# A hybrid decoder trunk on one core: near and far softmax parts weighted in their probabilities instead of in their outputs

## What is computed

```
def dilated_band_attention(q, k, v, bias, dilation):
    ...
    logits = jnp.where(key_ok[None, :, None, None, None, :], logits, NEG_INF)
    lse = jax.nn.logsumexp(logits, axis=-1)
    probs = jnp.exp(logits - lse[..., None]).astype(v.dtype)
    out = jnp.einsum('bnrhic,bncrhe->bnirhe', probs, vband).reshape(B, s_pad, H, Dh)[:, :S]
    ...
def dilated_attention_mixer(h, w_qkv, q_gain, k_gain, w_o, rel_bias):
    ...
    weights = jax.nn.softmax(jnp.stack(lses), axis=0)
    o = jnp.sum(weights[..., None] * jnp.stack(outs).astype(jnp.float32), axis=0)
    return o.reshape(B, S, ATTN_HEADS * ATTN_HEAD_DIM).astype(h.dtype) @ w_o
```

## Time and profile before

| | us |
|---|---|
| median of 3 runs | 1822.7 |
| lowest, highest | 1820.6, 1823.12 |
| the profiled execution: its time | 1820.68 |
| its span, first to last instruction | 1818.9 |
| PE busy | 1791.6 (99%) |
| DVE busy, ACT busy | 875.0 (48%), 759.4 (42%) |

### The profile page before, as it was taken

How to read it: one execution, slowest core, us unless ns; L and a number is a source line. 1 busy time by engine, 2 the same in 40 slices (tenths; PEclk the granted TensorE clock), 3 DMA queues, 4 the chain that set the end, 5 groups by cost and what they waited for, 6 DMA issues and landing times.

```text
span 1818.9 us, 36160 instructions
## 1 busy us (share of the span) xinstructions
PE 1791.6 (99%) x15618; PEld 1366.8 (75%) x15618; DVE 875.0 (48%) x1515; ACT 759.4 (42%) x1292; POOL 197.1 (11%) x172
## 2 busy tenths in 40 slices
PE   8999999999999999999999999999999999999999
PEld 3746666666478888888887887887887788888887
DVE  6724444454364444333455555555555544444322
ACT  4434444432242222222556656656657532323221
POOL 0033334331100000000111011111110000000000
PEclk9999999999999999999999999999999999999999
DMA  3321222131123323332232222222222233223332
GB/s 107 117 67 54 84 67 67 64 99 55 59 90 104 93 93 99 99 104 93 93 93 70 82 82 70 82 82 70 82 82 70 63 95 98 93 95 103 101 97 93
DMA packets 57541, 155.00 MB, mean 85 GB/s; under 512 B 5591, under 2 KB 22535, under 8 KB 57384
## 3 DMA queue, kind: packets, MB, share of 16 engines
q1 hardware_dynamic: 57288, 152.63, 26.4%
q10 hardware_dynamic: 96, 0.07, 0.0%
HBM read 150.51 MB, written 11.61 MB: 89 GB/s over the span
## 4 chain that ended last, share of the span: by engine, by line
PE 91%; ACT 4%; DVE 2%; issue 1%; POOL 1%; DMA 0%; ACTq 0%; DVEq 0%; POOLq 0%
PE bank L573 89%; PE bank L576 3%; ACT f L1597 2%; DVE f L2122 0%; DVE r L1994 0%; ACT f L1584 0%; ACT f L1610 0%; DVE f L1724 0%; DVE f L1727 0%; ACT r L1575 0%; DVE f L1744 0%; ACT r L1287 0%; DMA f<-const 0%; ACT f L1571 0%; DVE r L1750 0%
## 5 line engine op out<-in xcount | busy, mean ns | idle before, releaser
L573 PE MATMUL bank<-r 128*128 128x512 f32 x5424 | 1255.8, 391 | 2.7 <-DVE r L1994 1.1
L573 PEld LDWEIGHTS bank<-r 128*128 128x128 f32 x5424 | 1011.9, 188 | 226.0 <-issue 10.7
L573 PE MATMUL bank<-f 64*64 64x64 f32 (+5 forms) x9762 | 502.2, 255 | 16.0 <-ACT f L1312 4.3
L1701 DVE TENSOR_TENSOR r<-f,r 128x1024 fp32r<-128x1024 f32 x222 | 274.9, 1239 | 397.2 <-ACT r L1287 397.2
L573 PEld LDWEIGHTS bank<-f 64*64 64x64 f32 (+3 forms) x9762 | 306.9, 140 | 200.6 <-issue 128.0
L1287 ACT ACTIVATE r<-f 128x1024 fp32r<-128x1024 f32 x222 | 232.5, 1048 | 147.1 <-PE bank L573 141.5
L2314 POOL TENSOR_TENSOR r<-f,r 128x512 fp32r<-128x512 f32 x48 | 62.2, 1296 | 839.1 <-ACT r L1575 839.1
L1554 ACT ACTIVATE r<-f 128x512 fp32r<-128x512 f32 x44 | 27.8, 632 | 215.6 <-DVE f L2033 215.6
L2063 DVE TENSOR_TENSOR f<-bank,f 128x512 f32<-128x512 f32 x72 | 56.2, 781 | 73.3 <-PE bank L573 70.0
L1551 ACT ACTIVATE f<-f 128x512 f32<-128x512 f32 x44 | 27.8, 632 | 110.5 <-DVE f L2023 110.5
L1584 ACT ACTIVATE f<-bank,f 128x512 f32<-128x512 f32 x48 | 32.9, 686 | 94.8 <-PE bank L573 94.8
(11 more groups left out here) (106 smaller groups left out, 909.9 us busy)
## 6 DMA issues: line engine op xcount, KB each, us to landing
f<-stream SPq DMA_DIRECT2D x246, 512.0 KB, 3.4
bias_copies<-bias_rows SPq DMA_DIRECT2D x6, 1536.0 KB
f<-xT SPq DMA_DIRECT2D x16, 256.0 KB, 4.8
f<-lora_out SPq DMA_DIRECT2D x16, 128.0 KB, 6.4
f<-bias_copies SPq DMA_DIRECT2D x16, 128.0 KB, 3.2
f<-bias_copies SPq DMA_DIRECT2D x32, 64.0 KB, 2.9
outT<-f SPq DMA_DIRECT2D x8, 256.0 KB, 4.3
f<-const SPq DMA_DIRECT2D x1, 576.0 KB, 3.8
```

The source lines that it names most:

```text
L573: return nc.tensor.matmul(out, lhsT, rhs, start=start, stop=stop, skip_group_check=True)
L1701: TT(r(lo_at(q), 1024), f(O_RAW + panel_of(q) % RAW * 1024, 1024), rf(hi_at(q), 1024), ALU.subtract).then_inc(s["w_lo"], 1)
```

## The change

The two parts are weighted before they meet V, in the factor that the probabilities are multiplied with anyway. With own and other log-sum it is 1 / (sum * (1 + exp(other - own))). `attend` sums both into bank 6.

- A query's near log-sum lies in a tile of queries in a row, its far one in a tile of one residue. The near queries are now stored in the order (block, residue, index): `norm_projection` writes query group 0 in four instructions instead of one, SP loads its bias in four transfers of 32 partitions instead of one, and `attend` writes the far part as runs of 32.
- `total` (DVE, i = 5, ahead of everything of that step) makes all 16 log-sums of the pair at once. `exchange_lse` (PE, visit 5) takes the place of `lse_difference`: 4 matmuls with 128 x 128 weights and 16 columns each instead of 16 with 128 columns. `other_lse` (DVE, i = 5) is seven small instructions, each waiting for the one before, `weights` (ACT) one Exp, `scales` (DVE) two more. `normalize` of both halves stands behind them, at i = 5 and 6, where it stood at i = 2 and 4.
- Flips go through two banks, 5 and 7, one for a head; both heads of a group stand together. Flips and attends move: visits 6 and 7 flip groups 0 and 1, visit 8 attends 0 and 1 and flips group 2, visit 0 of the next iteration flips group 3, its visit 1 attends 2 and 3. Visit 4 is empty. Flips and attends now fill five visits (6, 7, 8, 0, 1).
- The sigmoid, its two table loads for an iteration, the copy `keep_near` and the three steps of the old `combine` go; ACT and DVE read bank 6 directly for high and low part.

```diff
-            def lse_difference(hp):
+            def exchange_lse(hp):
                 fill_att(4, "lse", hp)
...
-                for n in range(2 * NT):
-                    for h in range(2):
-                        lo = HD * h
-                        o = banks[4][lo:lo + HD, n * P:(n + 1) * P] if n < NT else \
-                            banks[4][lo:lo + HD, n - NT:S:4]
-                        last = mm(o, bc(f(O_SM + 40 * h + 32 + n, 1), (0, HD)), con(C_ID), n == 0, False)
+                pe.wait_ge(s["lse"], hp + 1)
...
+                for c in range(4):
+                    last = mm(banks[4][:, 16 * c:16 * (c + 1)], f(O_E4 + c * P, P), bc(f(O_SM + 32, 48), (40, 2), (1, 8)))
                 last.then_inc(s["lse_ps"], 1)
...
-                    if 3 <= i <= 6:
-                        flip_probs(a, 0, i - 3)
+                    if i == 0 and b >= 0:
+                        flip_probs(b, 3)
                     if i < 4:
                         logits(a, i)
-                    if 4 <= i <= 7:
-                        attend(a, i - 4)
-                    if 3 <= i <= 6:
-                        flip_probs(a, 1, i - 3)
-                    if i == 7:
-                        lse_difference(a)
+                    if i == 1 and b >= 0:
+                        attend(b, 2)
+                        attend(b, 3)
+                    if i == 5:
+                        exchange_lse(a)
+                    if i in (6, 7):
+                        flip_probs(a, i - 6)
+                    if i == 8:
+                        attend(a, 0)
+                        attend(a, 1)
+                        flip_probs(a, 2)
...
+            def weights(hp):
+                act.wait_ge(s["ex_step"], 7 * hp + 6)
+                A(f(O_EX + 112, 16), f(O_EX + 112, 16), ACT.Exp).then_inc(s["ex_exp"], 1)
...
+            def other_lse(hp):
+
+                def step(ins, n):
+                    ins.then_inc(s["ex_step"], 1)
+                    dve.wait_ge(s["ex_step"], 7 * hp + n)
+
+                dve.wait_ge(s["lse_ps"], hp + 1)
+                att_free(TT(bc(f(O_EX, 64), (4, 16), (1, 4)), banks[4][:, 0:64].rearrange("p (u n) -> p u n", n=4),
+                            bc(f(O_SM + 80, 4), (0, 16), (1, 4)), ALU.mult), 4)
+                att_read(dve, 4, "lse", hp)
+                step(TT(bc(f(O_EX + 64, 32), (2, 16), (1, 2)), bc(f(O_EX, 62), (4, 16), (1, 2)),
+                        bc(f(O_EX + 2, 62), (4, 16), (1, 2)), ALU.add), 1)
+                step(TT(f(O_EX + 96, 16), bc(f(O_EX + 64, 31), (2, 16)), bc(f(O_EX + 65, 31), (2, 16)), ALU.add), 2)
...
+                step(TS(f(O_EX + 112, 16), f(O_EX + 112, 16), 80.0, None, ALU.min), 5)
+                TS(f(O_EX + 112, 16), f(O_EX + 112, 16), -80.0, None, ALU.max).then_inc(s["ex_step"], 1)
...
             for it in range(NHP):
-                a = it - 1
+                a, b = it - 1, it - 2
                 for i in range(9):
+                    if a >= 0 and i == 5:
+                        total(a)
                     split_low(p_of(T_QKV + 9 * it + i) + LEAD)
                     take_projection(it, i)
                     if i:
                         norm_projection(it, i - 1)
...
-                    if i in (2, 4):
+                    if i == 3 and b >= 0:
+                        combine_low(b)
+                    if i == 5:
+                        other_lse(a)
+                        scales(a)
+                    if i in (5, 6):
                         for h in range(2):
-                            normalize(a, h, i // 2 - 1)
+                            normalize(a, h, i - 5)
```

More of the change, by code:

```diff
@@ L1146, in block_of, with flip_probs @@
                 return O_P + h * 4 * S + (n + (4 if kind == "B" else 0)) * 2 * P + e * P
[L1148 to L1153, removed]
+            def flip_probs(hp, g):
+                for h in range(2):
+                    b = 5 + 2 * h
+                    fill_att(b, g, hp)
+                    pe.wait_ge(s[f"probs{h}"], 8 * hp + (4 if g < 2 else 8))
+                    for j, what in enumerate(GROUPS[g]):
+                        last = flip(banks[b][:, j * P:(j + 1) * P], f(block_of(h, what), P))
+                    last.then_inc(s["flipped"], 1)
@@ L1625, in keep_near, with keep_both @@
[L1625 to L1630, removed]
+            def keep_both(a, g):
+                for h in range(2):
+                    keep_flipped(a, h, g)
             for it in range(NHP):
-                a = it - 1
+                a, b = it - 1, it - 2
                 for i in range(9):
[L1635 to L1640, removed]
+                    split_high(p_of(T_QKV + 9 * it + i) + LEAD)
@@ L1647, in _ @@
                         continue
[L1648 to L1651, removed]
+                    if i == 2 and b >= 0:
+                        combine(b)
                     if i in (2, 4):
@@ L1654, in _ @@
                             exps(a, h, i // 2 - 1)
[L1655 to L1659, removed]
+                    if i == 5:
+                        weights(a)
+                    if i == 8:
+                        keep_both(a, 2)
             def last_pair(a):
                 projection_aux(a, 8)
+                keep_both(a - 1, 3)
                 split_high(PAN_WO1 + 3)
+                combine(a - 1)
                 exps(a, 0, 0)
@@ L2074, in norm_projection @@
                     if hp >= 2 and g == 0:
-                        dve.wait_ge(s["attended"], 4 * (hp - 1))
+                        for h in range(2):
+                            dve.wait_ge(s[f"logits{h}"], 4 * (hp - 1))
                     to = O_QN + (hp % 2 * 6 + g * 2 + kind) * S
@@ L2080, in norm_projection @@
                             bc(f(O_QS), (4, P), (1, 4)), ALU.mult, ALU.mult).then_inc(s["qk_norm"], 1)
+                    elif kind == 0:
+                        for c in range(4):
+                            part = lambda off: bc(f(off + c, S - 3), (P, 4), (4, 32))
+                            last = STT(bc(f(to + 32 * c, S - 96), (P, 4), (1, 32)), part(O_QR + n % 2 * S), gain,
+                                       part(O_QS), ALU.mult, ALU.mult)
+                        last.then_inc(s["qk_norm"], 1)
                     else:
@@ L2152, in _ @@
                         continue
-                    if i == 0 and a:
-                        combine(a - 1)
                     if i < 4:
@@ L2183, in last_pair @@
                 negate_max(a, 1, 1)
-                normalize(a, 1, 0)
-                combine(a - 1)
-                normalize(a, 0, 1)
                 split_low(PAN_WO1 + 4)
-                normalize(a, 1, 1)
-                combine_low(a - 1)
-                combine(a)
+                total(a)
+                other_lse(a)
+                scales(a)
+                for half in range(2):
+                    for h in range(2):
+                        normalize(a, h, half)
                 combine_low(a)
```

183 lines of the change are left out of this document (88 added, 95 removed).

## The result

The changed kernel takes 1837.65 us (median of 4 runs, 1835.06 to 1840.76) against 1821.65 (1820.31 to 1823.12): ratio 1.008, 95% interval 1.0066 to 1.0095; the medians stand 16.0 us apart. The forecast was no change (1822.3, range 1815.6 to 1829.5). One rival had the right sign (small steps that cost more, slower), but not the mechanism.

What follows compares the result with a forecast made beforehand. PE, busy 1791.6 of 1818.9 us, was taken as the bound. Stretch 1 -14.4, rest of iterations +13.3, first pair -0.84, last iteration -2.25, last pair +3.8 made -0.4 us: 1822.3, no change, range 1815.6 to 1829.5.

Steps and rivals of the forecast that it cites:

- small steps that cost more: Rival, DVE/ACT chain: ten steps at 0.3 us each, +7 us, 1829.3; decides from 0.06 a step; chance 0.27.
- The logarithms on ACT: Stretch 1, both heads' Ln on ACT: ready 13.36 us after the start of product 4.
- The whole chain of ten: Dependent small steps from `other_lse` to the multiplications: seven on DVE, ACT's Exp, two more; T + 17.49 to T + 19.54.
- the flips' price: Exchange in visit 5: flips at 0.11 us each would make 0.87, the upper end; 0.65 was taken.
- -0.4 was forecast: Whole kernel: sum of all terms, -14.4 + 13.3 - 0.84 - 2.25 + 3.8 = -0.4 us.
- the savings named: Per iteration: 16 matmuls less exchange 1.1 us, old wait 0.6, fewer changes between dense, flip and attend some 0.65.
- the two waits of 2.75: New PE waits per iteration, for the exchange (1.79 us) and the multiplications (0.96), taking back the savings.
- 68.5 against 68.35: Length of one attention iteration in us, forecast for the changed kernel against that of the kernel before.
- stretch 1: Product 4's start to product 7's: 22.12 us in place of 24.18, -2.06 in each of seven iterations, -14.4.
- PE starts 0.15 after DVE's end: Stretch 1, visit 5: `total` ends at T + 13.56, so PE starts the exchange at T + 13.71.
- the second wait: Visit 6: PE waits 0.96 us, in two parts, for the multiplications of heads 0 and 1.
- waits of 1.79: Visit 5: PE waits 1.79 us for the exchange, since the visit 4 that covered this is empty.

Runs made afterwards that it cites:

- both causes out: Changed kernel with the exchange writing bank 5 instead of 4 and five needless dense matmuls ahead of it: 1824.08 us, ratio 1.0006.
- the two filled kernels: Changed kernel with ten needless dense matmuls ahead of the exchange, 1826.82 us; changed kernel with exchange in bank 5 and five such matmuls, 1824.08 us.
- the three kernels with cover: Changed kernel, older pair's two attends moved from visit 1 to 5: 1818.50 us; also exchange in bank 5: 1813.85; also product 4's norm behind near-half multiplications: 1810.56.
- the kernel with the other bank: Changed kernel with one edit, the exchange writes bank 5 instead of bank 4: 1828.22 us, ratio 1.0033.
- two others: Changed kernel with product 4's norm ahead of step 5's split on ACT, 1833.55 us; kernel before with a bare PE wait added behind visit 4, 1848.45 us.
- the other kernel: Kernel before with a PE wait for ACT's first far-half exponential added behind visit 4: 1848.45 us bare, 1836.58 with nine needless matmuls ahead of the wait.

## Why the prediction was wrong

**What held.** The logarithms on ACT were forecast 13.36 after product 4 and ended at 13.38 (1169.85). `total` was forecast to end at 13.56; it starts at 13.48 and ends at 13.65. The multiplications on DVE were forecast from 19.54 and start at 19.65 (1176.12). The small steps take 0.17 to 0.25 us, seven of them 1.5. The whole chain of ten took 2.31 (1173.81 to 1176.12) where 2.05 were forecast, 0.03 a step more, and began 0.15 early; the rival of dearer steps needed 0.06 a step and falls. The exchange cost 0.91 and not 0.65, at the flips' price. With both causes out the order costs +1.1 us where -0.4 was forecast. One sum doesn't come out: the savings named beside the two waits of 2.75 (1.1, 0.6 and 0.65) make 2.35, where 68.5 against 68.35 asks for 2.6. Nothing else was worked out from it.

**The step that failed is in stretch 1: "PE starts 0.15 after DVE's end".** It took the log-sums for the only thing that the exchange waits for. The code names a second, `fill_att(4, ...)`. In the kernel before it had cost nothing, but not because the bank was long free: in visit 7 `lse_difference` stood behind a norm too, that of product 6. There eight attends lay between (1111.90 + 1.03 = 1112.93), and ACT had been idle and read the bank at once, until 1112.69:

```profile
1112.00 0.69 ACT L1584 ACTIVATE f<-bank,f 128x512 f32<-128x512 f32 x1 [2.66 <-PE bank L573]
```

In visit 5 nothing lies between, and ACT reaches the norm's Ln only behind its exponentials and a split. The wait was 2.85 and not 1.79. Of the difference the second wait (0.96 forecast, 0 in the seven iterations) gave most back, and at full clock product 7 came 22.66 after product 4 instead of 22.12: some 3 us by the two filled kernels.

**The term that was missing is the clock: 11.9 us of the 16** by the medians (16.0 less 4.1), 10 of 14.6 by the ratios; their intervals leave some 3 us either way. The prediction counted a microsecond of waiting as a microsecond. It had the earlier trace rows with PE's waits at 0.62 and wrote down waits of 1.79 without asking whether a length is reached from which PE comes back slower. Among the kernels here the seven waits and the profiled execution's mean clock go together: 0.3 to 0.9 us with 0.998 or 0.999, 1.7 to 3.1 with 0.992 to 0.994, and between them the three kernels with cover (0.996 to 0.998), whose first iteration still waits for 1.8 or 2.7. It is not a rule for the single wait: behind 2.85 the clock fell in some iterations and not in others, and behind 1.16 it fell once. A wait of 1.79, as forecast, would have cost already: the kernel with the other bank has that wait, and with it filled by five matmuls it is 4.1 us faster (1828.22 and 1824.08, beside 1822.72 and 1823.01 for the kernel before).

The two causes don't simply add. With bank 4 the clock costs 11.9 us, with bank 5 only 4.1, since there a second wait takes up half of a slow product 6. So the bank alone is worth 3.0 with the clock held up and 9.4 without. With either of the two out the time would have been inside the stated range (1828.22 and 1826.82).

**That the new waits take back what the order saves** was right within what can be told: at full clock, with the other bank, an iteration takes 68.80 us, where 68.5 were forecast and 68.35 stood before. A way out was in the same paragraphs: visit 4 was emptied, while visit 1 got 16 attends that wait for nobody. Put ahead of the exchange they take 11.5 us of waiting (20.1 to 8.6) and most of the clock's share with it.

## What to carry to other kernels

Of a step that is moved, list every wait in front of it, the one for the buffer that it writes above all, and look up who used that buffer last at the new place, and what the engine that frees it has to do first. Where PE is busy all the time, price a new wait twice, once for itself and once for the clock behind it, less what a later wait takes up; needless matmuls in the wait tell in one experiment how much is the clock. And if an order has a wait of known length, move into it work that is ready.

## What the runs showed of the hardware

A PE that is 98% busy, and at full clock in the rest of the attention stage, ran dense matmuls at 1.2 GHz for part of the run behind a single wait of 1.7 to 3.1 us: in four of seven iterations of the changed kernel's profile, in five with the other bank, in six in each of two others. Behind waits of 0.3 to 0.95 us it never did, behind one of 1.16 it did once. It costs 11.9 us here, four times what the longer wait itself did, and 11.9 us again in the other kernel. It costs less where another wait follows: a product of 7.13 us instead of 5.71 cost nothing in front of two waits of 1.46 together. Ten needless matmuls of 0.23 us in an iteration made it 10.8 us faster (1837.65 and 1826.82). Four fp32 matmuls of 16 columns against 128 x 128 weights took 0.91 us, about as long as eight transposes of 128 columns (0.96).
